# Both feed-forwards of a two-block network by one level of Strassen's algorithm

## The reference, cut to what matters

```python
D_FF = 2816
def swiglu(h, w_gate_up, w_down):          # h [tokens, 1024], w_gate_up [1024, 5632], w_down [2816, 1024]
    gu = h @ w_gate_up
    gate, up = jnp.split(gu, 2, axis=-1)
    return (jax.nn.silu(gate) * up) @ w_down
hs = hs + rms_norm(swiglu(h, w_gate_up[layer], w_down[layer]), norm_ffn_post[layer])
```

## Time and profile before

| | |
|---|---|
| median of 3 runs | 2831.42 us (2828.78 to 2837.12) |
| span of the profiled execution, first to last instruction | 2827.2 us |
| its own time outside the span | not given by itself; the median lies 4.2 us above the span |
| PE busy | 2655.4 us, 94% of the span |
| DVE busy | 1234.2 us, 44% |
| ACT busy | 782.9 us, 28% |
| mean granted TensorE clock | 0.974 of full speed |
| layer 0's feed-forward | from 93.8 us to 895.7 us of the span |
| layer 1's feed-forward | from 1275.5 us to 2042.7 us |

### The profile page before, as it was taken

The page is one execution under the profiler, slowest core; times in us unless marked ns, Lnnn a source line. Parts: engine busy times, 40 slices in busy tenths (PEclk is TensorE's granted clock), DMA queues, the critical chain, the costliest instruction groups (busy, mean ns, idle before and its releaser), DMA issues. The chain is left out here.

```text
span 2827.2 us, 47951 instructions
## 1 busy us (share of the span) xinstructions
PE 2655.4 (94%) x20165; PEld 2210.2 (78%) x20165; DVE 1234.2 (44%) x2074; ACT 782.9 (28%) x1483; POOL 248.0 (9%) x175
## 2 busy tenths in 40 slices
PE   9899999999998999989999999999799999688778
PEld 8899999999986866667888888887677777577656
DVE  6433333333334458462333333333624464444366
ACT  6321111111126249442121111111322422233231
POOL 2100000000002025100000000000600000222110
PEclk9999999999998999999999999999899999899979
DMA  6311111111114500322111111111310211100132
GB/s 181 98 45 45 45 45 45 45 45 45 45 60 166 187 35 2 97 104 86 45 45 49 60 47 45 45 45 54 134 58 26 97 53 67 44 5 4 42 118 93
DMA packets 62950, 183.52 MB, mean 65 GB/s; under 512 B 10581, under 2 KB 19062, under 8 KB 61246
## 3 DMA queue, kind: packets, MB, share of 16 engines
q1 hardware_dynamic: 62784, 181.12, 19.1%
HBM read 150.48 MB, written 30.03 MB: 64 GB/s over the span
## 5 line engine op out<-in xcount | busy, mean ns | idle before, releaser
L812 DVE TENSOR_TENSOR f1hf<-f1sg,f1gu 128x512 f32<-128x512 f32 x44 | 30.3, 688 | 336.9 <-ACT f1sg L759 336.9
L812 DVE TENSOR_TENSOR f0hf<-f0sg,f0gu 128x346 f32<-128x346 f32 (+1 forms) x66 | 34.1, 517 | 327.6 <-ACT f0sg L759 327.6
L860 PE MATMUL f0gu<-b1XH,f0w0H 128*128 128x346 f32 (+1 forms) x528 | 170.5, 323 | 4.7 <-DVE f0w0L L792 4.1
L823 DVE TENSOR_TENSOR Y<-f0dn,Y 128x512 f32<-128x512 f32 (+1 forms) x180 | 124.0, 689 | 113.7 <-PE f0dn L907 112.7
L862 PE MATMUL f0gu<-b1XH,f0w0L 128*128 128x346 f32 (+1 forms) x528 | 171.1, 324 | 0.0
L861 PE MATMUL f0gu<-b1XL,f0w0H 128*128 128x346 f32 (+1 forms) x528 | 170.5, 323 | 0.0
L862 PE MATMUL f0gu<-b1XH,f0w1L 128*128 128x346 f32 (+1 forms) x528 | 170.2, 322 | 0.0
L861 PE MATMUL f0gu<-b1XL,f0w1H 128*128 128x346 f32 (+1 forms) x528 | 169.7, 321 | 0.0
L860 PE MATMUL f0gu<-b1XH,f0w1H 128*128 128x346 f32 (+1 forms) x528 | 169.0, 320 | 0.0
L823 DVE TENSOR_TENSOR Y<-f1dn,Y 128x512 f32<-128x512 f32 x160 | 109.3, 690 | 88.8 <-PE f1dn L907 88.8
L860 PE MATMUL f1gu<-b1XH,f1w0H 128*128 128x512 f32 x352 | 139.5, 396 | 3.2 <-DVE f1w0L L792 3.2
(11 more groups left out here) (430 smaller groups left out, 6605.8 us busy)
## 6 DMA issues: line engine op xcount, KB each, us to landing
f0raw<-in_w_gate_up SPq DMA_DIRECT2D x43, 512.0 KB, 5.8
f1raw<-in_w_gate_up SPq DMA_DIRECT2D x43, 512.0 KB, 5.7
residual<-Y SPq DMA_DIRECT2D x32, 512.0 KB, 2.8
Y<-in_w_ada SPq DMA_DIRECT2D x8, 1536.0 KB, 6.4
f0rawd<-in_w_down SPq DMA_DIRECT2D x22, 512.0 KB, 3.2
f1rawd<-in_w_down SPq DMA_DIRECT2D x22, 512.0 KB, 3.3
w_in_b_raw<-in_w_in_b SPq DMA_DIRECT2D x16, 512.0 KB, 3.3
w_in_a_raw<-in_w_in SPq DMA_DIRECT2D x11, 512.0 KB, 4.2
```

The lines of the kernel that those rows point to most:

```text
L812: dve.tensor_tensor(hf[:, i, 0:w], sg[:, i, 0:w], gu[:, i, 1, 0:w], ALU.mult).then_inc(s["mul"], 1)
L823: dve.tensor_tensor(y, dn[0:r, (par * ND + i) % 4], y, ALU.add).then_inc(s["acc"], 1)
L860: pe.matmul(o, wH[c][:, j, k], xh, start=(k == 0), stop=False)
```

## The change

`ffn_stage` is replaced by `strassen_ffn` in both layers.

**Gate and up.** With the four operand quarters (gate or up rows; channels in halves of 4 chunks; tokens in halves of 520 in layer 0, 512 in layer 1) each q but the first two is made in 7 products of 4 chunks in place of 8. A product is 4 chunks × NS slices × 3 matmuls: NS is 2 with 260 tokens in layer 0, 1 with 512 in layer 1. The weight sums are made per q by DVE (`made_sums`), the input sums once by DVE; ACT rounds 7 quarters (`high_piece`), DVE subtracts 7 (`low_piece`). Three PSUM groups are used, and partial results are copied out by ACT and added by DVE between products. q 0 and 1 are made in the former way (`classical_part`) while the input sums are built. The hidden values aren't kept in SBUF: `store` writes them to DRAM.

**Down.** Contraction (2 × 11 q), tokens (2 × 4 tiles) and features (2 × 512) are halved. The 7 products P1, P5, P6, P3, P7, P2, P4 have 11 steps each; a step is 12 matmuls of 128x512 (4 tiles × 3). For each step SP loads 2 or 3 blocks of 256 KB from DRAM, DVE forms up to two sums, ACT rounds, DVE subtracts, into a ring of R = 5 slots; a slot is loaded again when PE has finished the step that used it. The last 5 steps of P4 are run tile after tile, after all of them are split.

**Meta tokens (layer 0).** Their down product is made in plain fp32, 2 matmuls of 128 by 16 against 512 columns for each q, into four strips of 32 PSUM partitions that are added up by 4 small matmuls at the end.

```diff
@@ strassen_ffn: loads and sums of a down step
+            return {
+                "P5": [(sa, hidden_tiles(j, 1)), (KS[:, j], hidden_tiles(k2, 1)), (sb_, down(j, 1))],
+                "P6": [(KA[:, j], hidden_tiles(j, 0)), (sa, down(k2, 1))],
+                "P3": [(ra, hidden_tiles(k2, 0)), (rb, down(k2, 1))],
+                "P7": [(sa, hidden_tiles(j, 1)), (rb, down(k2, 1)), (sb_, down(j, 1))],
+                "P2": [(ra, hidden_tiles(k2, 0)), (rb, down(k2, 0))],
+                "P4": [(ra, hidden_tiles(k2, 1)), (rb, down(k2, 0))],
+            }[p]
...
+                "P1": [],
+                "P5": [(KS[:, j], KS[:, j], sa, ALU.add), (KB[:, j], sb_, KB[:, j], ALU.subtract)],
+                "P6": [(KS[:, j], KS[:, j], KA[:, j], ALU.subtract), (KB[:, j], sa, KB[:, j], ALU.subtract)],
+                "P3": [(ra, ra, KS[:, j], ALU.subtract)],
+                "P7": [(ra, KA[:, j], sa, ALU.subtract), (rb, rb, sb_, ALU.subtract)],
+                "P2": [],
+                "P4": [(rb, rb, KB[:, j], ALU.subtract)],
@@ ACT, then DVE, for a down step
+                def step_high(n):
+                    if sums(n):
+                        act.wait_ge(s["ad"], made[n + 1])
+                    act.wait_ge(s_ld[n % R], landed_at[n])
+                    for x, a in sources(n):
+                        act.activation(ring[:, n % R, 2 + x.start:2 + x.stop], a, ACT.Copy).then_inc(s["h2"], 1)
+                def step_low(n):
+                    todo = sums(n)
+                    dve.wait_ge(s_ld[n % R], landed_at[n])
+                    for dst, x, y, op in todo:
+                        dve.tensor_tensor(dst, x, y, op).then_inc(s["ad"], 1)
+                    at_h = split_at[n]
+                    for x, a in sources(n):
+                        at_h += 1
+                        dve.wait_ge(s["h2"], at_h)
+                        dve.tensor_tensor(ring[:, n % R, x], a, ring[:, n % R, 2 + x.start:2 + x.stop].bitcast(f32), ALU.subtract).then_inc(s["l2"], 1)
@@ PE, one q of gate and up (waits for copies and sums between the products)
+                    product(0, par, a, True)
+                    pe.wait_ge(s["c"], 3 * i)
+                    product(1, par, C_GROUP, True)
...
+                    pe.wait_ge(s["cp"], 3 * i + 1)
+                    product(2, par, a, False)
+                    pe.wait_ge(s["cp"], 3 * i + 2)
+                    product(3, par, C_GROUP, False)
+                    pe.wait_ge(s["cp"], 3 * i + 3)
+                    product(4, par, a, False)
+                    pe.wait_ge(s["c"], 3 * i + 1)
+                    product(5, par, C_GROUP, True)
+                    pe.wait_ge(s["c"], 3 * i + 2)
+                    product(6, par, a, False)
@@ PE, the down steps; OUTER = 72, P4_FIRST = 66, EARLY = 5 (layer 0) or 4, FIRST_TILE = 1 or 0
+                for n in range(OUTER):
...
+                    if n >= OUTER - 3 - FIRST_TILE:
+                        tail.tensor(pe, n - (OUTER - 3 - FIRST_TILE))
+                pe.wait_ge(s["l2"], split_at[-1])
+                for t in range(4):
+                    for n in range(OUTER, len(steps)):
+                        mm = tile(n, t, bank_a[t], False, n == len(steps) - 1)
+                    mm.then_inc(s["pd"], 1)
+                    if t == 2:
+                        tail.tensor(pe, EARLY - 1)
@@ SP, the last product
+                for n in range(P4_FIRST, len(steps)):
+                    step_loads(n)
+                    if n >= P4_FIRST + R - FIRST_TILE and kept < EARLY:
+                        tail.keep(sp, kept)
+                        tail.load(sp, kept + tail.loads)
+                        kept += 1
```

More of the change, by code:

```diff
@@ L152, in __init__ @@
         self.fetched = 0
+        with ExitStack() as rounded:
+            self.Y_rounded = self.sb(rounded, "Y_rounded", [P, (NT + 1) * D], f32r)
         self.Y = self.sb(ctx, "Y", [P, NT + 1, D])
@@ L196, in alloc_x @@
     def alloc_x(self, ctx, name, tokens, side="left"):
+        with ExitStack() as plain:
+            self.XH_plain = self.sb(plain, name + "XH_plain", [P, KC, tokens], f32, side)
+            self.XL_plain = self.sb(plain, name + "XL_plain", [P, KC, tokens], f32, side)
         self.XH = self.sb(ctx, name + "XH", [P, KC, tokens], f32r, side)
@@ L474, in __init__ @@
     def __init__(self, b, ctx, name, tiles, residual, store, post_gain, pre_gain=None, modulate=None, cols=None,
-                 ready=None, junk=None, sole=False, loads=2, slots=2, lag_2=2, lag_h=3, lag_l=None):
+                 ready=None, junk=None, tp=None, sole=False, loads=2, slots=2, lag_2=2, lag_h=3, lag_l=None):
         self.b, self.tiles, self.residual, self.store = b, tiles, residual, store
@@ L490, in __init__ @@
         self.st = b.sb(ctx, name + "st", [P, 6, 9])
-        self.tp = b.ps(ctx, name + "tp", [P, slots, KC, P])
+        self.tp = tp if tp is not None else b.ps(ctx, name + "tp", [P, slots, KC, P])
         names = [f"rx{i}" for i in range(loads)] + ["gains", "ss1", "sd1", "r1", "xg", "x", "ss2", "sd2", "r2", "xn", "tp", "xh", "xl", "stored"]
@@ L2805, in fetch_keys @@
                 b.fetched += 1
-            ffn_stage(b, fetch_keys, "f0", 0, TILES_META, SLICES_META, 2, lambda ctx, ready: Tail(
+            strassen_ffn(b, fetch_keys, "f0", 0, META, 2, lambda ctx, ready, tp: Tail(
                 b, ctx, "p1", TILES_META, lambda t: b.res[0][TILES_META[t][0]:TILES_META[t][0] + TILES_META[t][1], :], b.res[1], ins["norm_ffn_post"][0], lag_2=1, lag_h=2, lag_l=3,
-                cols=lambda t: slice(P * (t - 1), P * t) if t else slice(SEQ, TOK), ready=ready))
+                cols=lambda t: slice(P * (t - 1), P * t) if t else slice(SEQ, TOK), ready=ready, tp=tp))
             ada_rows = nc.dram_tensor("ada_rows", [1, 3 * D], f32, kind="Internal").ap()
@@ L2813, in program @@
             shift, scale1 = (ada_rows[0, D * i:D * (i + 1)] for i in range(2))
-            ffn_stage(b, lambda sp: b.fetch_first(sp, ins["w_in_2"][0:P, 512:1024]), "f1", 1, TILES_SEQ, SLICES_SEQ, 3, lambda ctx, ready: Tail(
-                b, ctx, "p3", TILES_SEQ, lambda t: x3[P * t:P * (t + 1), :], x4, ins["norm_ffn_post"][1], modulate=(scale1, shift), lag_2=1, lag_h=3, lag_l=4, ready=ready))
+            strassen_ffn(b, lambda sp: b.fetch_first(sp, ins["w_in_2"][0:P, 512:1024]), "f1", 1, 0, 1, lambda ctx, ready, tp: Tail(
+                b, ctx, "p3", TILES_SEQ, lambda t: x3[P * t:P * (t + 1), :], x4, ins["norm_ffn_post"][1], modulate=(scale1, shift), lag_2=1, lag_h=2, lag_l=3, ready=ready, tp=tp))
             second_block(b, x4, ada_rows, first)
```

589 lines of the change are left out of this document (added).

## The result

The changed kernel takes 2793.15 us (median of 4 runs, 2787.81 to 2797.59) where the kernel before took 2832.28 beside it: a ratio of 0.9862 (95% interval 0.9841 to 0.9882), 39 us faster. Five more runs of it on another occasion gave 2784.18 us and 0.9838 (0.9821 to 0.9855). The forecast was 2738 us, with a range from 2695 to 2785: the sign was right, and more than half of the gain of 94 us is missing.

What follows compares the result with a forecast made beforehand. PE, busy 94% of the time, was taken as the bound: 2831.4 us less 198.7 for fewer matmuls plus 105 for chain, tail, entry, clock and meta tokens gave 2737.7 us, range 2695 to 2785.

Steps and rivals of the forecast that it cites:

- entry, and clock there: Start of the down product: 3.0 us before step 0 (0.9 before in layer 0), plus slow matmuls after the wait.
- Matmul prices and what PE saves: Both layers: 0.121 us per 260-column matmul, 0.232 per 512; fewer matmuls in gate, up and down save 198.7 us.
- Gate and up hidden at nothing: Gate and up: DVE's and ACT's waits between products cost nothing, hidden behind PE's 19.5 us a q.
- Meta tokens: Layer 0: 44 plain fp32 matmuls, pairs side by side, cost 9.5 us; 18.9 if serial, 4.7 if four together.
- Down, the new chain: Down steps: DVE and ACT take turns, 3.18 us in P5, P6, 2.93 in P3, P4, 3.53 in P7; +17.6 a layer.
- The DMA rival: Down steps bound by loads; no longer faster at 302 us a stage, 157 GB/s; 2860 us at 150 GB/s; 4 in 100.
- The clock rival: Down steps with sums: PE's small idle brings the lower clock, +88 us a layer, 2914 us; 2 in 100.
- The rule of the Trainium skill about micro-idles: Down steps: micro-idles between matmul groups can make the clock swing; weighed for the clock rival, the trace so far disagreeing.
- Tail: End of each down product: splits and tail tiles take turns, PE stands; +28 and +26 us, less 4.8 in layer 1.
- A link: Tail: one split to the next, through ACT, DVE, POOL and loads; step 71 at 14.0 us, 72 at 19.7 in layer 0.
- Clock: After a long wait some 10 matmuls cost 0.2 us more each; about 1.5 times a layer, +3 us each.
- The 2.4: Meta tokens: the skill's 2.38 times for three column tiles would make the meta matmuls some 8 us, an estimate.

Runs made afterwards that it cites:

- e3: Changed kernel with ACT copying the meta tokens' four strips ahead of its step 6 instead of step 10; 0.9796 of the kernel before.
- e10: e7 plus SP storing the second hidden chunk before its wait for the first meta matmuls; 2720.34 us, 0.9608 of the kernel before.
- e6: Changed kernel with ACT and DVE splitting down steps 0 and 1 before they finish the last q; 0.9797 of the kernel before.
- e4: Changed kernel with DVE making the next down step's sums before it subtracts for the current one; 0.9735 of the kernel before.
- e5: Changed kernel with SP issuing a tail step's loads ahead of the tile's store and residual load; 0.9781 of the kernel before.
- e9: e7 with early tail tiles squared, scaled and added on only 8 of 1024 columns, the rest left out; 0.9539 of the kernel before.
- e7: Changed kernel with the edits of e3, e4, e5 and e6 together; 2727.86 us, 0.9616 of the kernel before.

## Why the prediction was wrong, by its own steps

Table 2: the terms in us for each layer; measured by the starts in the trace or by the run named.

| term | layer 0 forecast | measured | layer 1 forecast | measured |
|---|---|---|---|---|
| gate and up saving | −51.2 | −55.4 | −55.7 | −58.6 |
| down saving | −61.2 | −65.6 | −30.6 | −35.1 |
| meta pairs and the strips' sum | 9.5 | 13.1 + 2.2 | | |
| wait for the strips | none | 10.5 (e3) | | |
| wait at the start | none | 4.4 (e10) | | |
| entry, and clock there | 2.1 + 1.5 | 6.1 (e6: 3.8 gone) | 3.0 + 1.5 | 4.7 (e6: 2.8 gone) |
| chain in P5 to P7 | 17.6 | 21.3 (e4: 13.2 gone) | 17.6 | 23.3 (e4: 12.4 gone) |
| tail, and clock there | 28 + 1.5 | 42.3 | 26 − 4.8 + 1.5 | 40.0 |
| stage | −52.2 | −20.5 | −41.5 | −31.1 |

The measured stages are the means of the traces with the same code. A down step without a wait takes 2.72 us, 0.2267 us a matmul, where the kernel before has 0.2315 (25.0 us for 108), and the down saving, the entry, the chain and the tail are counted from that. The measured rows sum to −21.1 and −25.7: layer 0 closes within 1 us, layer 1 misses by 5. Of these the kernel before accounts for a part: its last step waits 2.89 and 2.84 us, with slow matmuls behind each, where 4.8 was counted. The rest isn't placed.

**Matmul prices and what PE saves: right, a little low.** A q saved 22.93 − 20.16 = 2.77 us in layer 0 and, from ACT's starts 19.37 us apart, 2.93 in layer 1. A step of the down product takes 2.72 us where 2.78 was forecast, so it saved over 4 us more a layer.

**Gate and up hidden at nothing: right** in the steady part (464 of 469 us busy, with the one wait in the 5 left) and wrong for the first q of layer 0. The queue of SP was the thing to follow: the fetch for the meta tokens, with its wait for PE, stood ahead of the stores that ACT's buffers wait for. 4.4 us.

**Meta tokens: mis-sized, and a wait overlooked.** A pair of q costs 21.35 − 20.16 = 1.19 us for its four matmuls, 13.1 in all against 9.5. They do run in pairs side by side, as forecast (two start within 0.02 us of each other, and the next two 0.42 later); what was left out are some 0.3 us a pair of q around them. The forecast priced the matmuls and never asked when ACT copies the strips out. That wait, with the matmuls at the lower of the two clock levels behind it, cost more than the matmuls' error: 10.5 us, shown by e3.

**Down, the new chain: right** in each step's length to 0.02 us. Over steps of 2.72 us the stalls are 4 and 6 us a layer more than forecast, and the cheaper matmuls take that back: steps 0 to 66 with the chain come to 203.5 and 205.5 us where the forecast has 204.1. The DMA rival had 157 GB/s as its limit; the window shows 210 with 0.67 of the engines' time. The clock rival has next to nothing: PEclk is 1.00 from 620 to 756 us in layer 0 and 0.99 from 1737 to 1880 in layer 1, where one step after a wait of 2.9 us ran slow (4.44 us). The rule of the Trainium skill about micro-idles that was weighed there ("TensorE: Matmul & The Clock Gate", A second HAM failure mode: psum-queue depth-cycling) doesn't show itself in this kernel.

**Tail: the step that failed.** The prediction let steps 71 to 74 be split "at 14.0, 19.7, 26.1 and 32.4" and 76 at 40.2 in layer 0, and in layer 1 at 10.9, 18.3, 24.4, 31.6 and 39.4. Counted from PE's end of step 66 (793.5 and 1904.65 us), they are split at 17.1, 24.2, 31.9, 39.0 and 48.7 in layer 0 and at 14.1, 24.0, 32.9, 41.5 and 50.4 in layer 1. The first and the last of them on DVE in layer 1 (steps 71 and 76):

```profile
1916.54 2.17 DVE L1470 TENSOR_TENSOR f1ring<-f1ring_plain,f1ring 128x1024 fp32r<-128x1024 f32 x1 [1.12 <-ACT f1ring L1309]
...
1953.81 1.22 DVE L1470 TENSOR_TENSOR f1ring<-f1ring_plain,f1ring 128x1024 fp32r<-128x1024 f32 x1 [1.12 <-ACT f1ring L1309]
```

The mechanism was right: splits and tiles take turns on ACT, DVE and POOL, and PE waits for the last split. The sizes were not. A link, from one split to the next, was 7.3 us on the mean in place of 6.1 (layer 0) and 9.1 in place of 6.9 (layer 1). Two causes are shown. The loads stood behind `keep` and landed late (DVE waited 10.4 and 5.5 us for them; e5: 9.1 and 3.8 us). And every DVE operation was priced as if POOL were idle: between the four adds and the last split DVE's instructions took 3.3 us more than alone in layer 0 and 7.9 in layer 1. The trace of the kernel before had this already, beside the POOL row of 3.25 us that the forecast did use: in layer 1's tail DVE's scaling, priced at 1.28, took 2.70 beside a POOL add.

```profile
2005.59 2.70 DVE L585 SCALAR_TENSOR_TENSOR Y<-Y,p3st,p3gpost 128x1024 f32<-128x1024 f32 x1
```

So PE lost 859.2 − 793.5 less 31.0 of work (ten steps and five transposed tiles), 34.7 us, in layer 0, and 1978.5 − 1904.65 less 30.4, 43.4 us, in layer 1, where 22.5 was forecast. After its last matmul, layer 0 needed 24.6 us against 17.0 before (6 more forecast, 7.6 measured), layer 1 21.4 against 20.1 (4 forecast, 1.4 measured). Together the tails cost 30 us more than forecast, the two overlooked waits 15, the chain 9, the meta matmuls 6 and the entries 3; the cheaper matmuls gave back 16 of it. That is 47 us, against the 42 by which the two stages missed; the 5 between them are the part of table 2 that doesn't close.

**Clock: right in kind.** Behind each of five waits in layer 0's down product 6 to 14 matmuls cost 0.43 us, where such a wait was counted one and a half times a layer.

What of the tail's cost isn't shown: of the 82 us in both layers e5 took away 13, e9 26, and the order of PE and the size of the last block 5. Some 38 us stay. They are not the landings, for which DVE waits only 0.5 and 0.9 us in e7; 9 of them, by the changed kernel's trace, stand behind the last matmul. Whether the others are the hand-overs or the order in which ACT and DVE take splits and tiles was not tried by itself.

## What to carry to other kernels

An overlap of several engines is not priced by adding each engine's own durations: price DVE beside a busy POOL by rows where both run. Giving POOL's adds to another engine would be the edit to try; no run here did it. When a change adds a small part (here the strips and their fetches), follow its instructions through the queue of every engine and ask what stands behind each wait; two such waits (15 us) cost as much as all the arithmetic of that part. When edits act inside stages, compare the stages' lengths rather than the whole time: they repeat within 1.2 us in layer 0 and 3.4 in layer 1, where the whole moves by 10.

## What the runs showed of the hardware

Not expected: the mutual blocking of DVE and POOL (0.69 us becomes 2.83, and POOL's add of 2.3 becomes 3.2). Four plain fp32 matmuls of 128x16 against 512 columns, two by two on different strips of 32 partitions, cost 1.19 us together, 0.30 each, where 128x128 ones cost 0.43: 1.4 times. The 2.4 that was weighed in the prediction is for three side by side, and here there were two. Eight small fp32 matmuls of 16x16 against 512 columns cost 2.16 us at the upper clock level and 3.88 after a wait of 6.7 us. And the last stages of the unchanged kernel lasted 782.2 us in one execution and 795.6 in another.
